# Folding the gate weight into the value weight, and running the short convolution, its activation and the query projection head by head

## The reference, cut to what matters

```python
u = h @ w_in
x_m, z, glu_a, glu_b = split(u)                     # four parts of 1024 channels
x_c = silu(causal_depthwise_conv(x_m, w_conv_m, b_conv_m))       # 4 taps
q = einsum("bthd,hde->bthe", x_c per head, w_q)     # 4 heads of 256
k = einsum("bthd,hde->bthe", x_c per head, w_k)
v = einsum("bthd,hde->bthe", x_m per head, w_v)
gates = concat_per_head(q, k, v) @ w_gates + b_gates             # 8 columns: 4 input, 4 forget
ig, lf = gates[:4], log_sigmoid(gates[4:])
h_m = sigmoid(z) * group_norm(mlstm(q, k * Dh**-0.5, v, ig, lf))
a   = silu(group_norm(causal_depthwise_conv(glu_a * sigmoid(glu_b), w_dw, b_dw)))   # 31 taps
y   = concat(h_m, a) @ w_out
```

## Time and profile before

| | |
|---|---|
| the profiled execution | 2212.45 us |
| its span | 2210.7 us, 21077 instructions |
| busy, share of the span | PE 89%, DVE 48%, ACT 22%, POOL 14% |
| mean granted clock of PE | 0.96 |
| chain that ended last, by engine | PE 63%, DVE 16%, transfers 15%, ACT 4% |

### The profile page before, as it was taken

How to read it: one execution, slowest core, us unless ns; L and a number is a source line. 1 busy time by engine, 2 the same in 40 slices (tenths; PEclk the granted TensorE clock), 3 DMA queues, 4 the chain that set the end, 5 groups by cost and what they waited for, 6 DMA issues and landing times.

```text
span 2210.7 us, 21077 instructions
## 1 busy us (share of the span) xinstructions
PE 1966.2 (89%) x8022; PEld 1445.8 (65%) x8022; DVE 1055.6 (48%) x2562; ACT 492.0 (22%) x1192; POOL 313.4 (14%) x325
## 2 busy tenths in 40 slices
PE   4999899999999899999999999988778878888776
PEld 4876688888876687888899777777334434433232
DVE  6993566401794422001200322224776676777754
ACT  2023221101123222110010344212222222213222
POOL 1000001000000000000000000000444344444441
PEclk9999999999999999999998999999899999999999
DMA  9611179844431143449332222234999999999996
GB/s 401 263 40 72 58 267 415 351 152 150 171 117 39 40 175 124 152 139 277 142 134 94 98 77 77 77 133 147 422 422 421 421 421 409 421 421 421 422 421 275
DMA packets 71140, 512.69 MB, mean 232 GB/s; under 512 B 8064, under 2 KB 8320, under 8 KB 11264
## 3 DMA queue, kind: packets, MB, share of 16 engines
q0 software_dynamic: 45376, 322.98, 36.5%
q1 hardware_dynamic: 25664, 188.36, 22.8%
HBM read 506.07 MB, written 5.24 MB: 231 GB/s over the span
## 4 chain that ended last, share of the span: by engine, by line
PE 63%; DVE 16%; DMA 15%; ACT 4%; issue 1%; POOL 0%; SPq 0%; DVEq 0%; ACTq 0%; POOLq 0%
DMA region<-in_peer_uv,small 13%; PE pj L528 10%; PE pj L725 10%; PE pj L710 9%; PE st L940 8%; DVE region L1385 7%; PE pj L658 5%; PE pj L541 3%; PE pj L915 2%; DVE region L1708 2%; PE pj L563 2%; PE pj L737 1%; PE pj L754 1%; PE ms L774 1%; PE pj L843 1%
## 5 line engine op out<-in xcount | busy, mean ns | idle before, releaser
L940 PE MATMUL st<-region 128*128 128x512 f32 x940 | 445.5, 625 | 131.9 <-ACT region L1268 131.9
L940 PEld LDWEIGHTS st<-region 128*128 128x128 f32 x940 | 179.3, 198 | 391.1 <-ACT region L1268 196.4
L528 PE MATMUL pj<-hT,ring 128*128 128x256 f32 x1792 | 393.4, 381 | 1.0 <-ACT region L1106 1.0
L528 PEld LDWEIGHTS pj<-hT,ring 128*128 128x128 f32 x1792 | 341.2, 191 | 49.3 <-ACT region L1106 1.8
L1708 DVE CUSTOM_DVE_ANT_0 region<-region 128x1024 f32<-128x1024 f32 x235 | 285.4, 1222 | 121.5 <-DMA region<-in_peer_uv,small 118.3
L453 POOL DMA_INDIRECT region<-in_peer_uv,small x235 | 256.2, 1090 | 411.6 <-PE st L940 324.5
L710 PE MATMUL pj<-region,ring 128*128 128x256 f32 x1024 | 222.1, 379 | 3.6 <-ACT region L1106 2.7
L710 PEld LDWEIGHTS pj<-region,ring 128*128 128x128 f32 x1024 | 194.2, 190 | 31.9 <-ACT region L1106 3.5
L1385 DVE SCALAR_TENSOR_TENSOR region<-region,pc 128x255 f32<-128x255 f32 (+20 forms) x528 | 202.1, 462 | 0.0
L1268 ACT ACTIVATE region<-ident,small 128x128 f32<-128x128 f32 x256 | 88.8, 394 | 391.8 <-DVE small L1716 391.8
L1410 DVE CUSTOM_DVE_ANT_0 region<-region 128x1024 f32<-128x1024 f32 x96 | 112.9, 1221 | 54.2 <-DMA region<-in_ada_rest 41.1
(11 more groups left out here) (305 smaller groups left out, 1926.3 us busy)
## 6 DMA issues: line engine op xcount, KB each, us to landing
ring<-in_ring_w SPq DMA_DIRECT2D x162, 1024.0 KB, 4.8
region<-in_ada_rest POOLq DMA_DIRECT2D x40, 1024.0 KB, 12.5
region<-in_ada_first SPq DMA_DIRECT2D x4, 2048.0 KB, 17.6
region<-in_wqkv SPq DMA_DIRECT2D x2, 3072.0 KB, 12.1
bias_dram<-region POOLq DMA_DIRECT2D x1, 4096.0 KB, 46.2
region<-in_peer_uv,small POOLq DMA_INDIRECT x235, 16.5
region<-in_wcmp POOLq DMA_DIRECT2D x1, 2048.0 KB, 8.9
region<-bias_dram POOLq DMA_DIRECT2D x1, 2048.0 KB, 19.1
```

The lines of the kernel that those rows point to most:

```text
L528: i = nc.tensor.matmul(b[:, m, :], w[:, k, P * m:P * m + P], hT[:, k, :], start=(k == 0), stop=(k == CT - 1))
L940: i = nc.tensor.matmul(acc[:, u % 2, 512 * hf:512 * hf + 512], diag[:, m % NDIAG, :], uv[m % NBUF][:, D + 512 * hf:D + 512 * hf + 512], st ...
```

## The change

Per layer, the 16 matmuls that make channel-major v and their four drains go. In their place 16 matmuls with 8 moving columns multiply the transposed value weight (`wvT`, a new 1 MB input per layer, loaded into `tmp`) with the value part of the gate weights; ACT copies the 128 x 64 result to `wvg`, and 8 of the 24 gate matmuls use `wvg` against x_m in `U` in place of the gate weights against v. The wait of PE for the gate weights moves ahead, to the place of the new matmuls. The short convolution is written head by head (two tiles, four taps, next two tiles), the SiLU is cut in four, PE waits for each head's part before that head's q, and ACT drains the q of one head behind the SiLU of the next but one. Four fewer drains make the counts of `proj_drained` 60 per layer.

```diff
--- before.py
+++ after.py
@@ -133,6 +133,7 @@
     out["pe_cols"] = np.stack([np.concatenate([a[n][0].T, a[n][0].T]) for n in ("pe_k_2", "pe_v_2")], axis=1)
     out["x_cols"] = by_partition(a["x"][0].T).reshape(P, CT, T)
     out["wqkv"] = np.stack([np.stack([a[n][l].reshape(H * 2, P, DH).transpose(1, 0, 2) for n in ("w_q", "w_k", "w_v")], axis=1) for l in range(DEPTH)])
+    out["wvT"] = np.stack([by_partition(np.concatenate([w.T for w in a["w_v"][l]])) for l in range(DEPTH)])
     out["wg"] = np.stack([a["w_gates"][l].reshape(6, P, H, 2 * H).transpose(1, 0, 2, 3).reshape(P, 6, H * 2 * H) for l in range(DEPTH)])
     out["wgn"] = by_partition(a["w_in_2"][0][:, GN0:GN0 + 48]).reshape(P, CT, 48)
     cmp = [a[n][0].reshape(CMP_LEN, HD, HD).transpose(1, 0, 2) for n in ("w_cmp_k_2", "w_cmp_v_2")]
@@ -234,7 +235,7 @@
 
         y_acc, xy_acc, yg_acc, y_sq, yg_sq, xy = (tmp[:, k, :] for k in range(6))
         y_diag, x_diag = tmp[:, 6, :], tmp[:, 7, :]
-        vT = tmp
+        wvT = tmp[:, :, :]
         y = hT
 
         small = sb("small", [P, 3584])
@@ -247,6 +248,7 @@
         mod_scale = sb("mod_scale", [P, DEPTH, 4, CT])
         mod_sum = sb("mod_sum", [P, DEPTH * ADA_TILES])
         wg = sb("wg", [P, 6, H * 2 * H])
+        wvg = small_piece(1024, 2 * H * 2 * H)
         bg = sb("bg", [2 * H, 1])
         ident = sb("ident", [P, P])
         ones = sb("ones", [P, P])
@@ -324,7 +326,7 @@
             full_at.append(before + 16)
 
 
-        MERGE_BANKS, GATE_BANK, banks = [], None, 64 * DEPTH
+        MERGE_BANKS, GATE_BANK, banks = [], None, 60 * DEPTH
         for j in jobs[job_at[("kcmp", 2, 0)]:job_at[("vwin", 2, 0)] + 1]:
             banks += 1
         banks += 1
@@ -361,6 +363,8 @@
                     sp.wait_ge(sem("head_done"), H * l)
                 sp.dma_start(wqkv[:, :, :, :], a["wqkv"][l]).then_inc(sem("wqkv_in"), 16)
                 sp.dma_start(wg[:, :, :], a["wg"][l]).then_inc(sem("wg_in"), 16)
+                sp.wait_ge(sem("x_spread"), 2 * l + 1)
+                sp.dma_start(wvT, a["wvT"][l].rearrange("p (c d) -> p c d", d=DH)).then_inc(sem("wg_in"), 16)
                 sp.dma_start(bg[:, :], a["b_gates"][l].rearrange("(g o) -> g o", o=1)).then_inc(sem("wg_in"), 16)
 
 
@@ -554,9 +558,18 @@
 
                 pe.wait_ge(sem("wqkv_in"), 16 * (l + 1))
                 pe.wait_ge(sem("proj_drained"), bank)
-
-                def heads_of(m, src):
+                pe.wait_ge(sem("wg_in"), 48 * (l + 1))
+                for c in range(2 * H):
+                    h, d = divmod(c, 2)
+                    for e in range(2):
+                        i = nc.tensor.matmul(ms[0][:, 0, 8 * c:8 * c + 8], wvT[:, 2 * h + e, P * d:P * d + P], wg[:, 4 + e, 8 * h:8 * h + 8],
+                                             start=(e == 0), stop=(e == 1))
+                i.then_inc(sem("wvg_made"), 1)
+
+                def heads_of(m, src, ready=None):
                     for h in range(H):
+                        if ready:
+                            pe.wait_ge(sem(ready), H * l + h + 1)
                         b = take_bank()
                         for e in range(2):
                             for d in range(2):
@@ -564,7 +577,6 @@
                                                      start=(d == 0), stop=(d == 1))
                         i.then_inc(sem("qkv_made"), 1)
 
-                heads_of(2, U)
                 for s in range(2):
                     for hp in range(2):
                         b = take_bank()
@@ -575,19 +587,19 @@
                                                      start=(d == 0), stop=(d == 1))
                         i.then_inc(sem("qkv_made"), 1)
                 wide("w_in", l, W_IN_ORDER[10:12])
-                pe.wait_ge(sem("xc_ready"), l + 1)
-                heads_of(0, xc)
+                heads_of(0, xc, "xc_ready")
                 heads_of(1, xc)
 
 
-                pe.wait_ge(sem("wg_in"), 32 * (l + 1))
                 pe.wait_ge(sem("proj_drained"), bank)
+                pe.wait_ge(sem("wvg_kept"), l + 1)
                 n = 0
-                for m, src in enumerate((qT, kT, vT)):
+                for m, src in enumerate((U, qT, kT)):
                     for e in range(2):
                         for h in range(H):
-                            i = nc.tensor.matmul(ms[0][0:2 * H, 0, :], wg[:, 2 * m + e, 8 * h:8 * h + 8], src[:, 2 * h + e, :],
-                                                 start=(n == 0), stop=(n == 23))
+                            c = 2 * h + e
+                            w = wg[:, 2 * (m - 1) + e, 8 * h:8 * h + 8] if m else wvg[:, 8 * c:8 * c + 8]
+                            i = nc.tensor.matmul(ms[0][0:2 * H, 0, :], w, src[:, c, :], start=(n == 0), stop=(n == 23))
                             n += 1
                 i.then_inc(sem("gates_made"), 1)
 
@@ -1035,22 +1047,25 @@
                 finish_h(l, 0)
                 drain_u(l, W_IN_ORDER[:10])
 
-                for h in range(H):
-                    drain(vT[:, 2 * h:2 * h + 2, :], ACT.Copy)
+                act.wait_ge(sem("wvg_made"), l + 1)
+                nc.scalar.copy(wvg, ms[0][:, 0, 0:64]).then_inc(sem("wvg_kept"), 1)
                 for s in range(2):
                     for hp in range(2):
                         drain(vtok[:, s, 512 * hp:512 * hp + 512].rearrange("p (a t) -> p a t", a=2), ACT.Copy)
                 drain_u(l, W_IN_ORDER[10:12])
-                act.wait_ge(sem("conv_m_ready"), l + 1)
-                nc.scalar.activation(xc[:, :, :], xc[:, :, :], ACT.Silu).then_inc(sem("xc_ready"), 1)
-                for dst in (qT, kT):
-                    for h in range(H):
-                        drain(dst[:, 2 * h:2 * h + 2, :], ACT.Copy)
+                for h in range(H):
+                    act.wait_ge(sem("conv_m_ready"), H * l + h + 1)
+                    nc.scalar.activation(xc[:, 2 * h:2 * h + 2, :], xc[:, 2 * h:2 * h + 2, :], ACT.Silu).then_inc(sem("xc_ready"), 1)
+                    if h:
+                        drain(qT[:, 2 * h - 2:2 * h, :], ACT.Copy)
+                drain(qT[:, 6:8, :], ACT.Copy)
+                for h in range(H):
+                    drain(kT[:, 2 * h:2 * h + 2, :], ACT.Copy)
 
 
                 act.wait_ge(sem("gates_made"), l + 1)
                 nc.scalar.activation(gates[:, :], ms[0][0:2 * H, 0, :], ACT.Identity, bias=bg[:, 0:1]).then_inc(sem("gates_kept"), 1)
-                act.wait_ge(sem("qkv_made"), 16 * (l + 1))
+                act.wait_ge(sem("qkv_made"), 12 * (l + 1))
                 act.wait_ge(sem("fg_moved"), l + 1)
                 link(nc.scalar.activation(fgr[:, 0, :], ms[0][0:H, 1, :], ACT.Copy))
                 link(nc.scalar.activation(fgr[:, 1, :], fgr[:, 0, :], ACT.Abs))
@@ -1391,16 +1406,17 @@
             def long_conv(l, pair):
 
                 a, b = U[:, 16 + 2 * pair:18 + 2 * pair, :], U[:, 24 + 2 * pair:26 + 2 * pair, :]
-                dve.wait_ge(sem("proj_drained"), 64 * l + (2 * pair + 2 if pair < 3 else 20))
+                dve.wait_ge(sem("proj_drained"), 60 * l + (2 * pair + 2 if pair < 3 else 16))
                 link(nc.vector.tensor_tensor(b, a, b, ALU.mult))
                 for back in range(KC):
                     tap(l, U[:, 16:24], U[:, 24:32], KC, W_DW, B_DW, back, (2 * pair, 2 * pair + 1), "conv_ready" if back == KC - 1 else None)
 
             def short_conv(l):
 
-                dve.wait_ge(sem("proj_drained"), 64 * l + 10)
-                for back in range(KM):
-                    tap(l, xc, U[:, 0:8], KM, W_CONV, B_CONV_M, back, range(CT), "conv_m_ready" if back == KM - 1 else None)
+                dve.wait_ge(sem("proj_drained"), 60 * l + 10)
+                for h in range(H):
+                    for back in range(KM):
+                        tap(l, xc, U[:, 0:8], KM, W_CONV, B_CONV_M, back, (2 * h, 2 * h + 1), "conv_m_ready" if back == KM - 1 else None)
 
             ada_at = 0
 
```

## The result

The changed kernel takes 2201.45 us (median of 6 runs, 2200.73 to 2203.67), the kernel before on the same chip 2213.48 us (6 runs, 2211.86 to 2216.93). The ratio is 0.9946, with a 95% interval of 0.9933 to 0.9959: 12 us faster. The forecast was 2204.9, in a range of 2197.5 to 2210.0. The forecast falls short of the gain by 3.5 us. Of the rivals, B (2200.9, one low clock stretch missing) comes nearest, nearer than the forecast itself.

A forecast was written before the change was run, and what follows sets the result against it. DVE's convolution, ACT's SiLU, then PE were taken to bound the stretch before the gates. Per layer 8.2 - 2.0 - 2.0 = 4.2 us, 8.4 for two, gave 2204.9 us against 2213.34, range 2197.5 to 2210.

The forecast's parts named there:

- B: Rival: one of the two low clock stretches per layer is missing, or they are in one layer only; 2200.9 us, chance 0.20.
- The bound before: Ahead of q, DVE's convolution and PE's path reach the SiLU nearly level; making only one shorter would bring little.
- The product, 3.6 us: At the start of the stretch, 16 matmuls of 8 columns take 3.6 us, in place of 6.98 us.
- The idle time, 2.6 us: PE idle from last w_in matmul to first q: drain, table load, a quarter of the SiLU and gaps, 2.6 us.
- q and k, 13.8 + 0.7: 64 records of q and k at full clock, 13.8 us, then last drain and hand-over to the gates, 0.7 us.
- the stretch at full clock: From the product's start to the first gate matmul, 41.6 us per layer, before any loss to the clock.
- The clock behind the product, 2.0 per layer: The narrow run brings the clock down, and wide work behind it loses 2.0 us per layer, bounds 0 and 3.3.
- By the busy share alone: Reading that the new product keeps the clock because PE never stands still in it; 2.0 us per layer better.
- The clock behind the idle time, 2.0 per layer: The clock falls at the 2.6 us of idle before q, costing 2.0 us per layer, bounds 0 and 3.3.
- Edits costed at nothing: New 1 MB load, convolution order, unchanged gate matmul count and DVE's later wait for the softplus cost 0 us.
- rival D: The new load is late and PE waits for it ahead of the whole stretch; slower, 2243 us, chance 0.03.
- Rival C: Clock still low when PE goes idle, rises late, both places cost 3.3 us; 2210.1 us, about no change, chance 0.14.

The follow-up runs named there:

- the product alone: The changed kernel with the short convolution, the single SiLU and the one wait ahead of q of the kernel before; 2214.52 us, ratio 0.9999.
- the heads alone: The kernel before with short convolution, SiLU, waits and q drains head by head, channel-major v kept; 2208.40 us, ratio 0.9970.
- the earlier SiLU: The changed kernel with the last two w_in blocks swapped, so table load and SiLU of heads 0 and 1 precede the last drain; 2197.55 us, ratio 0.9921.
- the product spread out: The changed kernel with its 16 narrow matmuls set in twos among token-major v groups and w_in half tiles; 2203.09 us, ratio 0.9949.
- the changed kernel's second execution: The changed kernel run again without an edit, beside later kernels; 2202.27 us, ratio 0.9944.
- one sixteenth: The changed kernel with one of the 16 narrow matmuls, read by all v gate matmuls, output not the reference's; 2197.05 us, ratio 0.9919.

## Why the prediction was right, and where it was off

*The bound before.* Right in the main. The prediction read the two paths into the SiLU as nearly level, so that making only one shorter brings little. For the product alone that held (0.9999). For the heads alone it was too strong, since they brought 6.3 us, half of the 12: the SiLU itself stands behind both paths, and the cut takes 1.3 us of it away whichever path is the longer.

*The product, 3.6 us.* Right: 3.56. The 48-column row was the right neighbour, and the copy (0.21 us at 112.52) lies beside token-major v.

*The idle time, 2.6 us.* Right: 2.63, released by ACT and not by DVE. DVE's last head ends at 139.0, and ACT starts its SiLU, which nothing of DVE's holds any more, at 143.26.

*q and k, 13.8 + 0.7.* Slightly short: 14.08 + 0.69 in layer 1, at full clock. With the other terms the stretch at full clock is 43.61 - 1.77 = 41.84 instead of 41.6. That is 0.5 us of gain less, for two layers.

*The clock behind the product, 2.0 per layer.* Right, and it is shown: the low stretch is there in all four layer passes of the changed kernel, and in the four of the product alone and the earlier SiLU. It is gone with the product spread out or nearly left out, with the same 0.73 us of idle time ahead. It cost 1.77. By the busy share alone the clock would have stayed, since that share was 1.00 in every whole microsecond from the start of the run to the fall.

*The clock behind the idle time, 2.0 per layer.* This is the term that was mis-sized. It came in one of four layer passes of the changed kernel and cost 1.4 us there (45.00 against 43.60); it began while PE still stood idle, and where it lay on q and k whole it cost 1.7 (15.77 against 14.08). The prediction took it from one row and charged it in both layers. Together, 8.0 us were charged to the clock and the profiled execution lost 2 x 1.77 + 1.4 = 4.9. The forecast of 8.4 us, plus these 3.1, minus the 0.5 above, makes the 11.0 that the stretches gave. The failing is that the two low stretches were added up as if each came whether or not the other did. Rival B, with one of the two missing per layer, is what three of the four layer passes show, and its 12.4 us are nearer to the measured 12.0 than the forecast's 8.4; it had a chance of 0.20. That the measured time lies inside the range owes something to the range having been made wide enough for B.

*What the trace of before could not tell.* Whether the clock falls at that place isn't set by the length of the idle time alone. With the same 2.63 us, it fell in both layers of three kernels (heads alone, product spread out, one sixteenth) and in neither of the changed kernel's second execution. Where the low stretch behind the product had come and the idle time was 2.63 us, the one ahead of q stayed away in three of four passes; with the 6.04 us of the product alone it came in both. That is seen in these executions. The kernels also differ in when the idle time falls (in layer 0 it begins between 128.7 and 136.6), and no run holds that fixed. What decides it isn't shown.

*Edits costed at nothing.* Right. The 0.73 us ahead of the product is no transfer's, and the same 0.73 us stood ahead of channel-major v, so the new load had landed (rival D is out). DVE still waited 6.75 and 5.37 us for the softplus; about 7 was said. Rival C asked for q and k as slow as before, and they were faster in both layers.

## What to carry to other kernels

Where two engines reach a meeting point at about the same time, price both halves of a change together: one alone may be worth nothing, as the product was. What stands behind the meeting point is worth shortening by itself, as the SiLU was. After each step read the chain again, since the holder changed three times here (DVE, then ACT with its table load, then DVE again, then PE alone). When a trace shows two places where the clock may fall, don't add their prices up without asking whether one replaces the other: here 3.6 us of 8-column matmuls cost 1.8 us behind them, and in three of four layer passes the 1.7 us further on, which were lost without them, then weren't. Taking the first low stretch away brought nothing while an idle time behind it was followed by another, and nothing while DVE held q.

## What the runs showed of the hardware

- Sixteen fp32 matmuls of 8 columns with 128 x 128 weights took 3.56 us, about the 3.60 of 48 columns. The weight loads beside them take 3.65 us for 32, so between these two widths it isn't the columns that set the time.
- The clock fell to 0.50 at the end of a run of sixteen such matmuls, 3.6 us long, with PE busy throughout, and stayed there for about 3.4 us; this came in eight of eight layer passes. In pairs (once four) between wide groups, the same sixteen left it at 1.00 in six of six.
- An idle time of 2.63 us ahead of q was followed by a low stretch in six of six layer passes with none just before it, and in one of four with one behind the product. What decides between them isn't shown.
- Profiled executions differ in parts that no edit touches: the stretch of layer 0 begins up to 1.6 us earlier or later, and 64 records of 256 columns take 14.08 us, or 15.77 where a low stretch lies on them.
